# Attention values stationary in two column groups, with transposed sums, and output weights scaled on GpSimd

## What is computed

```python
def finish_layer(x, attn, b_gate, conv_out, g_attn_out, g_conv_out, w_out, ...):
    a = rms_norm(attn.reshape(B_, T_, D_ATTN), g_attn_out)      # 12 heads x 64 = 768
    c = rms_norm(b_gate * conv_out, g_conv_out)                  # 256
    h = x + jnp.concatenate([a, c], axis=-1) @ w_out             # 1024 x 1024
    return h + hier_moe(rms_norm(h, g_norm_ffn), ...)            # 32 experts, 2 per token
...
def merge_by_denominator(parts):       # attention: sums of p*v over sums of p
    ...
    return num_t / den_t[..., None]
```

## Time and profile before

| | us |
|---|---|
| median of 3 runs | 610.65 |
| lowest and highest of them | 609.15, 611.22 |
| the profiled execution's own time | 607.84 |
| its span | 606.1 |
| TensorE matmuls busy | 553.9 (91%) |
| VectorE busy | 278.1 (46%) |
| ScalarE busy | 166.8 (28%) |
| GpSimd busy | 119.2 (20%) |
| HBM read and written | 151.06 MB and 19.76 MB, 282 GB/s over the span |

### The profile page before, as it was taken

One profiled execution on the slowest core, in us unless ns is written; L12 is line 12 of the kernel. 1 busy time (PEld: TensorE's weight loads), 2 busy tenths in 40 slices (PEclk: granted clock), 3 DMA queues, 4 the chain that ended last, 5 costly groups with the idle time before them and its releaser, 6 DMA issues.

```text
span 606.1 us, 8209 instructions
## 1 busy us (share of the span) xinstructions
PE 553.9 (91%) x2944; PEld 332.5 (55%) x2944; DVE 278.1 (46%) x681; ACT 166.8 (28%) x365; POOL 119.2 (20%) x124
## 2 busy tenths in 40 slices
PE   6999999998999999899999999999996869687992
PEld 4798899887675888744555853333332313232320
DVE  5887667968314787524358731111210111111256
ACT  7445344423312567610412210100100100000031
POOL 0488788310001000000000021111110111100013
PEclk9999999999999999899999999999997979898897
DMA  7990342599377900069600879999999999999874
GB/s 274 281 304 5 118 156 66 183 273 316 143 209 251 420 31 2 2 203 407 264 35 36 355 250 388 409 419 419 422 421 421 421 419 421 420 422 419 333 297 156
DMA packets 47159, 163.48 MB, mean 270 GB/s; under 512 B 8650, under 2 KB 22026, under 8 KB 35832
## 3 DMA queue, kind: packets, MB, share of 16 engines
q1 hardware_dynamic: 40448, 145.46, 63.2%
q0 software_dynamic: 6528, 17.01, 7.8%
q10 hardware_dynamic: 144, 0.52, 0.2%
HBM read 151.06 MB, written 19.76 MB: 282 GB/s over the span
## 4 chain that ended last, share of the span: by engine, by line
PE 47%; SPq 17%; DMA 11%; DVE 6%; POOL 3%; issue 3%; ACT 2%; POOLq 0%; DVEq 0%; ACTq 0%
SPq L512 11%; PE bank L1022 9%; PE bank L1085 9%; SPq L525 6%; DMA ring<-in_w_up_dram 5%; PE bank L1112 4%; PE bank L875 4%; DMA x<-q_rows 3%; PE bank L786 3%; PE bank L860 2%; DVE x L1445 2%; PE bank L808 2%; POOL ring L2139 2%; DMA hn_rows<-work 2%; PE bank L809 2%
## 5 line engine op out<-in xcount | busy, mean ns | idle before, releaser
L1085 PE MATMUL bank<-ring,work 128*64 128x512 f32 x512 | 122.8, 636 | 19.8 <-DMA ring<-in_w_up_dram 19.5
L1085 PEld LDWEIGHTS bank<-ring,work 128*64 128x64 f32 x512 | 39.6, 146 | 100.9 <-issue 87.1
L1445 DVE TENSOR_TENSOR work<-work,bank 128x256 f32<-128x256 f32 x16 | 6.7, 422 | 134.0 <-ACT work L1383 134.0
L1112 PE MATMUL bank<-ring,work 128*64 128x512 f32 x256 | 60.1, 612 | 7.6 <-ACT work L1387 7.6
L729 PE MATMUL bank<-split 128*128 128x384 f32 x192 | 66.1, 344 | 0.1
L730 PE MATMUL bank<-split 128*128 128x384 f32 x192 | 64.3, 335 | 0.0
L1022 PE MATMUL bank<-ring 128*128 128x512 f32 x96 | 42.6, 595 | 0.0
L1383 ACT ACTIVATE work<-bank 128x256 f32<-128x256 f32 x16 | 6.2, 385 | 128.2 <-PE bank L1085 128.2
L2139 POOL TENSOR_TENSOR ring<-ring 128x192 f32<-128x192 f32 (+1 forms) x40 | 38.8, 988 | 8.0 <-DVEq L1540 6.9
L1445 DVE TENSOR_TENSOR split<-ring,split 128x768 fp32r<-128x768 f32 (+1 forms) x35 | 37.3, 1099 | 6.4 <-PE bank L716 6.1
L1112 PEld LDWEIGHTS bank<-ring,work 128*64 128x64 f32 x256 | 17.3, 140 | 40.1 <-issue 28.7
(11 more groups left out here) (266 smaller groups left out, 832.9 us busy)
## 6 DMA issues: line engine op xcount, KB each, us to landing
ring<-in_w_down_dram SPq DMA_DIRECT2D x32, 1024.0 KB, 24.5
ring<-in_w_gate_dram SPq DMA_DIRECT2D x28, 1024.0 KB, 23.1
ring<-in_w_up_dram SPq DMA_DIRECT2D x28, 1024.0 KB, 25.2
ring<-in_w_in_dram SPq DMA_DIRECT2D x7, 1536.0 KB, 11.4
results<-work POOLq DMA_DIRECT2D x1, 4160.0 KB, 26.1
x<-in_x_prompt_dram SPq DMA_DIRECT2D x8, 512.0 KB, 13.1
ring<-in_w_out_dram SPq DMA_DIRECT2D x1, 4096.0 KB, 17.9
ring<-in_w_gate_dram SPq DMA_DIRECT2D x8, 512.0 KB, 13.2
```

Source lines behind the costliest of these rows:

```text
L1085: last = pe.matmul(bank[2][64 * h:64 * h + 64, :], xgT[:, k, 64 * h:64 * h + 64], gate_up[s][h][:, :, k, :], start=(k == 0), stop=(k == KD ...
L1112: last = pe.matmul(bank[4 + j][64 * h:64 * h + 64, :], hT[:, c, 64 * h:64 * h + 64], down[s][h][:, c, j * 512:(j + 1) * 512], start=(c == ...
L1445: return dve.tensor_tensor(out, a, b, op)
```

## The change

TensorE's value matmuls swap their operands: 64 columns of `v_rows` are stationary, and the 128 x 128 transposed probabilities move. The two heads of a unit write to partitions 0 to 63 and 64 to 127 of one PSUM bank, in turns, so the sums come out transposed (head dimension on partitions, queries in columns), as `attnT` needs them. `attn` and its 24 transposes are gone, and so are the 8 multiplications by the gain.

A transposed sum must be divided along its columns. VectorE now takes the reciprocal of the denominators spread over 2 x 64 columns (`rden`, 128 x 128, one instruction a unit, ahead of the copy of the second head's probabilities of that unit). TensorE transposes it into the same bank behind the values, ScalarE copies it out (`rden_t`), and VectorE multiplies the sums by it into `attnT`.

GpSimd scales `wout` by the gains of both parts (16 instructions of 128 x 512), squares every unit's 128 x 128 block of `attnT` and adds it to a sum for its tile, and adds the two halves of the conv values' squares once. TensorE turns these sums into norms by one-column matmuls against ones (`conv_squares`, `tile_squares`), those of tiles 3, 2, 1 at step `p == NU` of the attention loop, ahead of the last transposes, along with the transposes of the conv rows and of the sample tokens' rows; that of tile 0 between the two halves of the sample tokens' output projection, which uses banks 1 and 3 now. `square_tile` on ScalarE and the product of `yT` with its gain on VectorE are gone. SyncE's wait ahead of the expert slots is for `ssc_done` 2. `turn_scores` gets seven 128-column matmuls of the identity with itself into bank 6, ahead of its wait.

`pool_made(u)`, `copied(u)` and `normed(u)` count the semaphores: `pool_made(u)` is GpSimd's count when unit `u` has been squared and added.

```diff
-        attn = cut(ring, 6160, NT, DA)
+        square_sum = cut(ring, 6160, NT, P)
+        squared = cut(ring, 6672, 2, P)
+        rden = cut(ring, 6928, 2, 2, DH)
+        rden_t = cut(ring, 7184, 2, P)
         qT = cut(ring, SLOT, NP, SEQ)
         kT = cut(ring, SLOT + 3072, NP, SEQ)
         v_rows = cut(ring, SLOT + 6144, NT, DA)
...
+                keep_warm(7, bank[6])
...
+            def turn_conv():
+
+                pe.wait_ge(S["conv_done"], 1)
+                for h in range(2):
+                    pe.transpose(bank[0][0:2, h * P:(h + 1) * P], cuT[:, h, SEQ:SEQ + 2], ident[:, :])
+                    last = pe.transpose(bank[0][0:DEC, DC + h * P:DC + (h + 1) * P], cu_s[:, h, 2, :], ident[:, :])
+                last.then_inc(S["conv_turned"], 1)
+
+            def turn_samples():
+
+                pe.wait_ge(S["masked"], 2 * NU)
+                for k in range(NP):
+                    last = pe.transpose(bank[2][:, k * DEC:(k + 1) * DEC], attn_s[0:DEC, k * P:(k + 1) * P],
+                                        ident[0:DEC, 0:DEC])
+                last.then_inc(S["a_turned"], 1)
+
+            def conv_squares():
+
+                pe.wait_ge(S["pool_made"], pool_made(SUM_Y))
+                pe.wait_ge(S["wr_in"], 96)
+                for t in range(NT + 1):
+                    n = TILES[t]
+                    pe.matmul(bank[4][0:n, 64 + t:65 + t], ysq[:, 0, t * P:t * P + n], ones[:, 0:1], start=True, stop=True)
+
+            def tile_squares(t):
+
+                pe.wait_ge(S["pool_made"], pool_made(NP * (NT - t) - 1))
+                return pe.matmul(square_bank(t)[:, 80 + t:81 + t], square_sum[:, t, :], ones[:, 0:1], start=True, stop=True)
+
             for p in range(NU + 2):
                 if 1 <= p < NU:
                     prompt_scores(p)
+                if p == NU:
+                    pe.wait_ge(S["masked"], 2 * NU - 2)
+                    turn_conv()
+                    conv_squares()
+                    for t in (3, 2, 1):
+                        last = tile_squares(t)
+                    last.then_inc(S["ssc_done"], 1)
+                    turn_samples()
...
-                    for h in range(2):
-                        pe.wait_ge(S["p_evac_v" if h else "p_evac_a"], u + 1)
-                        for j in range(qt + 1):
-                            last = pe.matmul(bank[6 + u % 2][:, h * DH:(h + 1) * DH], probs_t[u % 2][h][:, j * P:(j + 1) * P],
-                                             v_rows[:, j, (2 * hp + h) * DH:(2 * hp + h + 1) * DH],
-                                             start=(j == 0), stop=(j == qt))
-                    last.then_inc(S["o_done"], 1)
...
-            for g in range(2 * NT + 1):
-                t = g // 2
-                if g >= 2:
-                    pe.wait_ge(S["a_evac"], g - 1)
-                if t < NT:
-                    pe.wait_ge(S["o_evac"], NP * NT)
-                    for k in range(3):
-                        o = (3 * (g % 2) + k) * P
-                        last = pe.transpose(bank[g % 2][:, k * P:(k + 1) * P], attn[:, t, o:o + P], ident[:, :])
...
-            pe.wait_ge(S["a_evac"], 2 * NT + 1)
-            pe.wait_ge(S["y_gained"], 1)
+                    pe.wait_ge(S["p_evac_v"], u + 1)
+                    pe.wait_ge(S["p_evac_a"], copied(u))
+                    for j in range(qt + 1):
+                        for h in range(2):
+                            pe.matmul(bank[6 + u % 2][h * DH:(h + 1) * DH, 0:P],
+                                      v_rows[:, j, (2 * hp + h) * DH:(2 * hp + h + 1) * DH],
+                                      probs_t[u % 2][h][:, j * P:(j + 1) * P], start=(j == 0), stop=(j == qt))
+                    pe.transpose(bank[6 + u % 2][:, P:2 * P], rden[:, u % 2, :, :].rearrange("p h d -> p (h d)"), ident[:, :])\
+                        .then_inc(S["o_done"], 1)
...
+            pe.wait_ge(S["pool_made"], pool_made(2 * KD))
+            pe.wait_ge(S["a_evac"], 1)
             for j in range(2):
+                if j == 1:
+                    tile_squares(0).then_inc(S["ssc_done"], 1)
...
+                else:
+                    pe.wait_ge(*((S["conv_evac"], 1), (S["opp_evac"], 1), (S["a_std"], 1), (S["opp_evac"], 2))[g])
...
+            for p in range(NU + 3):
...
-                if p >= 1:
+                if p >= 3:
+                    u = p - 3
+                    act.wait_ge(S["o_done"], u + 1)
+                    if u >= 2:
+                        act.wait_ge(S["o_evac"], u - 1)
+                    act.activation(rden_t[:, u % 2, :], bank[6 + u % 2][:, P:2 * P], ACT.Copy).then_inc(S["p_evac_a"], 1)
...
-                if p % NP == 4 and p > NP:
-                    square_tile(p // NP - 1)
...
+                if p == NU:
...
+                if p == 16:
+                    act.wait_ge(S["rows_out"], 48)
+                    act.activation(junk[0:DEC, 0:DA], attn_s[0:DEC, :], ACT.Square, accum_out=ssa[0:DEC, NT:NT + 1])\
...
-                if p == 14:
-                    dve.wait_ge(S["y_squared"], 1)
-                    tt(yT, yT, bc(gains[:, 14:16], 2, TOK, [P, 2, TOK]), ALU.mult).then_inc(S["y_gained"], 1)
...
+                    dve.reciprocal(rden[:, u % 2, :, :], bc(den[:, (2 * u) % 24:(2 * u) % 24 + 2], 2, DH, [P, 2, DH]))
                     dve.tensor_copy(probs_t[u % 2][1][:, 0:n], turn_bank[1][:, 0:n]).then_inc(S["p_evac_v"], 1)
...
+                if p == NU + 2:
+                    dve.wait_ge(S["a_turned"], 1)
+                    dve.tensor_copy(mixsT[:, 0:NP, 0:DEC], bank[2][:, 0:NP * DEC].rearrange("p (a b) -> p a b", a=NP))\
+                        .then_inc(S["a_evac"], 1)
...
-                    chain.step(dve.reciprocal(rden[u % 2], den[:, (2 * u) % 24:(2 * u) % 24 + 2]))
-                    tt(attn[:, qt, 2 * hp * DH:2 * (hp + 1) * DH].rearrange("p (a b) -> p a b", a=2),
-                       bank[6 + u % 2][:, 0:P].rearrange("p (a b) -> p a b", a=2),
-                       bc(rden[u % 2], 2, DH, [P, 2, DH]), ALU.mult).then_inc(S["o_evac"], 1)
+                    dve.wait_ge(S["p_evac_a"], normed(u))
+                    tt(attnT[:, hp, qt * P:(qt + 1) * P], bank[6 + u % 2][:, 0:P], rden_t[:, u % 2, :], ALU.mult)\
+                        .then_inc(S["o_evac"], 1)
...
-            for g in range(2 * NT + 1):
-                t = g // 2
-                dve.wait_ge(S["a_turned"], g + 1)
-                if t < NT:
-                    k = 3 * (g % 2)
-                    tt(attnT[:, k:k + 3, t * P:(t + 1) * P], bank[g % 2][:, 0:CW].rearrange("p (a b) -> p a b", a=3),
-                       bc(gains[:, 8 + k:11 + k], 2, P, [P, 3, P]), ALU.mult).then_inc(S["a_evac"], 1)
-                else:
-                    tt(mixsT[:, 0:NP, 0:DEC], bank[g % 2][:, 0:NP * DEC].rearrange("p (a b) -> p a b", a=NP),
-                       bc(gains[:, 8:8 + NP], 2, DEC, [P, NP, DEC]), ALU.mult).then_inc(S["a_evac"], 1)
...
+            made = Chain(pool, S["pool_made"])
+            pool.wait_ge(S["wout_in"], 16)
+            for u, (qt, hp) in enumerate(pair_units):
+                if u < 2 * KD:
+                    here = wout[:, u // 2, u % 2 * 512:(u % 2 + 1) * 512]
+                    made.put(pool.tensor_tensor(here, here, gains[:, 8 + u // 2:9 + u // 2].to_broadcast([P, 512]), ALU.mult))
+                pool.wait_ge(S["o_evac"], u + 1)
+                chunk = attnT[:, hp, qt * P:(qt + 1) * P]
+                if hp == 0:
+                    made.step(pool.tensor_tensor(square_sum[:, qt, :], chunk, chunk, ALU.mult))
+                else:
+                    made.step(pool.tensor_tensor(squared[:, u % 2, :], chunk, chunk, ALU.mult))
+                    made.step(pool.tensor_tensor(square_sum[:, qt, :], square_sum[:, qt, :], squared[:, u % 2, :], ALU.add))
+                if u == SUM_Y:
+                    pool.wait_ge(S["y_squared"], 1)
+                    made.put(pool.tensor_tensor(ysq[:, 0, :], ysq[:, 0, :], ysq[:, 1, :], ALU.add))
```

84 lines of the change are left out of this document (31 added, 53 removed).

## The result

The changed kernel takes 606.21 us in the median of 7 runs (603.18 to 607.73), the kernel before 610.65 (609.15 to 612.18): a ratio of 0.9936, 95% interval 0.9913 to 0.9959, so 2.5 to 5.3 us faster. The forecast was 612.8 with a chance of 0.25 for faster. The time lies inside the range of 605 to 618, the sign was wrong.

What follows compares the result with a forecast made beforehand. VectorE was taken to bound attention: 188.75 + 71.0 + 4.0 - 1.6 = 262.2 to the last product, 3.9 to the first output group, 1.7 for the clock: 267.8, 2.0 later. Median 610.65 + 2.1 = 612.8 us, range 605 to 618.

Steps and rivals of the forecast that it cites:

- the reciprocal, 1.15: VectorE's 128-column reciprocal in each of 24 attention units: holds the engine 1.15 us instead of 0.16, +23.8 us in all.
- The sum of VectorE's stage: VectorE's work in attention: 48.4 + 23.8 - 1.2 = 71.0 us, more than the stage lasts, so VectorE becomes the bound.
- TensorE's terms: TensorE in a 512-wide attention unit: value matmuls 0.95 us instead of 1.83, the whole unit 3.26 instead of 3.82.
- The rival of no overlap: Value matmuls on TensorE: column groups don't overlap, 1.83 us again, +2 more, 614.8; chance 0.04.
- The tail: From attention's last product to the first output group: a chain of 3.9 us, plus 1.7 for the clock.
- The clock's dip: Granted clock likely at half level on the dense halves and first output groups: up to 3.4 us, 1.7 taken.
- The block's wait at VectorE: At step `p == NU`, VectorE idles 1.9 us because TensorE's added block stands ahead of the last transposes.
- GpSimd held: GpSimd's scalings, squares and sums beside attention: 49 us of work, ending at 252 if never starved, so hidden.
- GpSimd's delay: Rival: GpSimd slowed beside VectorE on SBUF, 49 us become 75, first output group at 279, +13, 624; chance 0.08.
- The seven matmuls: Added TensorE matmuls, 1.6 us, put into a wait of 1.84: no effect, unless that wait is shorter.
- The milder slope: Rival: VectorE's reciprocal grows by 7 ns a column, 0.97 us held, -4.3, 608.5; chance 0.16.
- the cheap reciprocal: Rival: VectorE's wide reciprocal holds only 0.21 us and VectorE doesn't bound, -8.8, 601.9; chance 0.14.

Runs made afterwards that it cites:

- priced_at_1_15: The changed kernel with an added 44-column reciprocal per unit on VectorE, so a unit's reciprocals cost the predicted 1.15 us: 610.65 us, ratio 0.9994.

## Why the prediction was wrong

**The term that failed is the reciprocal, 1.15.** The prediction put the slope at 8.5 ns a column, from widths of 2 and 6, and gave 7 ns a chance of its own. It is 6.3, and 0.87 is held. The two rows behind the fit differ by 34 ns, and I carried their slope over thirty times the distance; the pair 5 to 6 had pointed to 5 ns. By the Trainium skill (VectorE: DVE Perf Modes, First, the fixed hardware budget) the divide has a repeat count of 8; read as eight cycles a column that gave an estimate of 8.3 ns. The trace disagrees with this reading: at the page's 0.96 GHz the measured 6.3 ns are 6 cycles. priced_at_1_15 shows what the term was worth: the last product 3.9 us later and the first output group 2.9; its time, 610.65, is the kernel before's, so with the price that I forecast the change would have gained nothing.

**The sum of VectorE's stage was too steep.** At the right price it gives 71.0 - 24 x 0.28 = 64.3 of work and 66.7 to the last product; the trace has 63.2 of work and 68.6. So with the price mended the sum errs the other way, by 1.9. VectorE's idle time was 5.7 instead of 2.4: 2.2 up to 252.10, and 3.5 behind it (2.28 for the last transposes and 1.19 for ScalarE's last copy, where I had 1.9 and 0.9). In the 512-wide units TensorE sets the pace (17.01 of 17.06), and VectorE has 1.0 us to spare. It is busy for 20.63 of 20.80 us in the 384-wide units, 13.58 of 14.25 in the 256-wide and 10.80 of 11.17 in the 128-wide ones, but busy is not yet the bound: of the 1.4, 1.7, 1.7 and 2.0 us that priced_at_1_15 adds in the steps of the four widths, 0.2, 1.3, 0.3 and 2.1 come through (the last up to the last product and partly in the dip). One sum over stages with different bounds gives a slope of 24 for each us of price; measured between 0.87 and 1.15 it was 3.9 / 0.28 = 14.

**TensorE's terms held.** Values 1.03 (0.95 forecast, bounds 0.88 and 1.83), unit 3.37 (3.26). The rival of no overlap fell; the alternation brings 0.48 a unit, the swap by itself 0.32.

**The tail held.** Last product to first group: 5.6 us forecast (3.9 and 1.7 for the clock), 5.66 measured. The clock's dip came as forecast and cost 3.64 - 1.92 = 1.7 on the first half. It was this half, up to 260.6, that the second half stood behind, and not GpSimd's last sum, which ended at 258.97; at the full clock the two would have ended together. The block's wait at VectorE, 2.28, was forecast at 1.9.

**GpSimd held.** 1052 ns for 512 columns (1.3 forecast), never late. What I had looked for only as GpSimd's delay was VectorE's: 1.2 us at the taps.

**The seven matmuls held** in what can be measured: nothing.

**From the profile to the median.** I forecast +2.1 for the median and got -4.4. Of these 6.5, 4.7 are the first output group (267.8 against 263.1). Of the other 1.8 the interval of the ratio, 1.4 either way, covers all but 0.4. The two profiled executions stand 2.8 under and 1.5 over their medians, the second with the 2.9 us of the dip at 340. Where the dips fall in the unprofiled runs no row shows. How much there is of them the mean clock of each run does: 0.967 over the 7 of after, 0.964 over the 106 of the kernel before that stand beside the experiments, which is some 40 and 44 us at the lower level. So over the runs after is not slower by its clock, whatever the one profile shows, and where the last 1.8 us are from stays open.

**The weighing.** The milder slope and the cheap reciprocal had 0.30 together, and I had written that the reciprocal "is the term that decides". Its bounds (0.21 to 1.30) gave both signs; the middle of the range that rows allow at a slope of 5 to 9.7 was 1.0, and I took 1.15. That the time still came to lie in the range of 605 to 618 is no merit of the sum: the range was wide enough to hold both signs.

## What to carry to other kernels

An operation whose cost is extrapolated far beyond the widths in the trace is a coin with two sides: spread its chance over the whole span of slopes that the rows allow, or design around it. Here a 2-column reciprocal and a copy were 3.5 us cheaper than the wide one.

Sum an engine's work stage by stage and take in each stage the larger of the engines' sums; a single sum turns slack in one stage into a bound in another. And when dense matmuls can be moved in time, look first at the granted clock where they will land: packing them closer put them into the dip here, and cost more than the waits that it removed. How much of that is the dip and how much the order itself is not separated.
